# Splitting a router's column sums and residual products around its count, with later row waits, another PSUM bank and no zero products ahead of x

## The reference

```python
# layer 1 (called e1 in the kernel): RMS norm, experts of width 256
x = x + mixed @ w_out
x = x + _hier_moe(_rmsnorm(x, norm_ffn_g), ...)
# layers 2 and 3 (e2, e3): layer norms, experts of width 512
for i in range(2):
    ...
    y = concatenate([y_mix, y_mem], axis=-1) @ w_o[i]
    x = layer_norm(DEEPNORM_ALPHA * x + y, ln1_g[i], ln1_b[i])
    f = hierarchical_moe(x, w_rg[i], b_rg[i], w_re[i], b_re[i], w_gate[i], w_up[i], w_down[i])
    x = layer_norm(DEEPNORM_ALPHA * x + f, ln2_g[i], ln2_b[i])
# hierarchical_moe: best of 4 groups, best 2 of its 8 experts by logits x @ [w_rg | w_re];
# every token's output is the weighted sum of its two experts' silu(x @ gate) * (x @ up) @ down
```

## Time and profile before

| | us |
|---|---|
| median of 3 runs | 1717.15 |
| lowest, highest | 1714.5, 1717.75 |
| the profiled execution | 1714.65 |
| its span, first to last instruction | 1712.9 |
| PE busy in the span | 1601.9 (94%) |
| DVE, ACT, POOL busy | 522.1, 273.3, 35.7 |
| DMA | 570.23 MB, mean 333 GB/s |
| chain that ended last, by engine | PE 63%, DMA 30%, DVE 3% |

### The profile page before, as it was taken

How to read it: one execution, slowest core, us unless ns; L and a number is a source line. 1 busy time by engine, 2 the same in 40 slices (tenths; PEclk the granted TensorE clock), 3 DMA queues, 4 the chain that set the end, 5 groups by cost and what they waited for, 6 DMA issues and landing times.

```text
span 1712.9 us, 30730 instructions
## 1 busy us (share of the span) xinstructions
PE 1601.9 (94%) x12513; PEld 800.3 (47%) x12518; DVE 522.1 (30%) x1178; ACT 273.3 (16%) x545; POOL 35.7 (2%) x78
## 2 busy tenths in 40 slices
PE   8998998977699999999999999999899999999997
PEld 5486765643367553434333333674434333333332
DVE  6986333111048452112121111414542111111113
ACT  2303111000035220101010100223211010001011
POOL 4000000010000000000000000000000000000000
PEclk9999999989899999999999999999999999999999
DMA  6323459999984089999999999831389999999996
GB/s 249 136 111 147 166 217 410 421 421 420 421 367 160 34 312 422 422 422 422 421 422 422 422 422 422 373 133 66 148 334 421 422 422 422 422 422 422 421 422 256
DMA packets 79527, 570.23 MB, mean 333 GB/s; under 512 B 8878, under 2 KB 12390, under 8 KB 14566
## 3 DMA queue, kind: packets, MB, share of 16 engines
q1 hardware_dynamic: 77750, 563.41, 80.1%
q10 hardware_dynamic: 1712, 5.92, 0.9%
HBM read 568.24 MB, written 1.05 MB: 332 GB/s over the span
## 4 chain that ended last, share of the span: by engine, by line
PE 63%; DMA 30%; DVE 3%; issue 2%; ACT 1%; SPq 1%; POOL 0%; DVEq 0%; PEldq 0%; POOLq 0%; ACTq 0%
DMA space<-in_e_up 30%; PE psum L1092 20%; PE psum L1131 8%; PE psum L897 5%; PE psum L834 5%; PE psum L842 4%; PE psum L1144 4%; PE psum L1014 3%; PE psum L1456 2%; PE psum L1416 1%; PE psum L1001 1%; PE psum L886 1%; PE psum L1467 1%; PE psum L1356 1%; PE psum L1222 1%
## 5 line engine op out<-in xcount | busy, mean ns | idle before, releaser
L1092 PE MATMUL psum<-space 128*32 (+1 forms) x5056 | 524.1, 566 | 53.0 <-DMA space<-in_e_up 49.0
L1092 PEld LDWEIGHTS psum<-space 128*32 128x32 f32 x5056 | 168.4, 113 | 394.7 <-issue 386.7
L1131 PE MATMUL psum<-space 128*32 128x512 f32 (+1 forms) x2304 | 257.1, 597 | 6.3 <-DMA space<-in_e_down 6.3
L2151 DVE TENSOR_TENSOR space<-space,psum 128x512 f32<-128x512 f32 (+1 forms) x40 | 25.4, 635 | 581.6 <-PE psum L1092 581.6
L1144 PE MATMUL psum<-space 128*128 128x512 f32 x320 | 150.4, 613 | 0.0
L1131 PEld LDWEIGHTS psum<-space 128*32 128x32 f32 x2304 | 71.7, 110 | 162.5 <-issue 162.5
L834 PE MATMUL psum<-xT,space 128*128 128x256 f32 x448 | 98.5, 380 | 3.0 <-ACT xT L1520 1.0
L1144 PEld LDWEIGHTS psum<-space 128*128 128x128 f32 x320 | 54.2, 189 | 96.6 <-issue 71.8
L2158 DVE COPY space<-psum 128x512 f32<-128x512 f32 x40 | 27.7, 691 | 231.6 <-PE psum L1131 231.6
L834 PEld LDWEIGHTS psum<-xT,space 128*128 128x128 f32 x448 | 84.6, 190 | 15.9 <-issue 4.6
L1014 PE MATMUL psum<-space,xT 128*128 128x128 bf16 x1024 | 89.4, 219 | 0.0
(11 more groups left out here) (399 smaller groups left out, 1411.4 us busy)
## 6 DMA issues: line engine op xcount, KB each, us to landing
space<-in_e_up SPq DMA_DIRECT2D x160, 1024.0 KB, 20.2
space<-in_e_down SPq DMA_DIRECT2D x160, 1024.0 KB, 20.4
space<-in_e_gate SPq DMA_DIRECT2D x156, 1024.0 KB, 21.1
space<-in_stream SPq DMA_DIRECT2D x25, 2048.0 KB, 15.4
rows<-in_rows ACTq DMA_DIRECT2D x9, 512.0 KB, 8.8
rows<-in_e_gate SPq DMA_DIRECT2D x4, 1024.0 KB, 25.9
space<-in_stream SPq DMA_DIRECT2D x3, 1024.0 KB, 9.6
x_sb<-in_x SPq DMA_DIRECT2D x2, 512.0 KB, 4.0
```

The source lines that it names most:

```text
L1092: last = mm(psum[r, 5 + g, 0:FW], xg[:, u, k, r], w, start=(k == 0), stop=(k == KD - 1))
L1131: last = mm(psum[r, (4, 7)[half], :], hT[:, f, r], w, start=(f == 0), stop=(f == F - 1))
```

## The change

Five edits. (1) The zero products ahead of x and behind the first transposes are gone, and POOL clears no_sum after alpha_id and not first. (2) The gain rows' transpose goes to bank 7; the alternation of banks 0 and 1 shifts by one from f on. (3) In the router the residual products are issued two and two, the first two behind the first token half's norm; the first set of column sums stands between them, the second set behind the ranks; fewer zero products follow (none in e1, three in e2, seven as before in e3); PE waits for banks 5 and 6 after the first gather, not ahead of it; ACT copies the sums after the bfloat16 part. (4) `residual_norm` waits for the rows ahead of the first centring. (5) DVE clears wcomb and rank after the differences.

```diff
@@ plan @@
     for n in range(2):
         use2("u", n)
+    use(("gains",), 7)
...
-    use2("gains")
     use2("f")
@@ gpsimd @@
-        step(po.memset(no_sum[:, :], 0.0))
-        finish(po, "pool", "no_sum")
         step(po.memset(ident[:, :], 0.0))
...
         finish(po, "pool", "alpha_id")
+        step(po.memset(no_sum[:, :], 0.0))
+        finish(po, "pool", "no_sum")
@@ tensor, moe @@
-            after(pe, "pool", "alpha_id")
-            if e != "e1":
-                after(pe, "vec", e + "_tok")
-            for b in range(4):
+            def residual_start(b):
+
                 pe.wait_ge(bank_free[b], before_moe[e][b])
                 mm(psum[:, b, :], (ident if e == "e1" else alpha_id)[:, :], x_sb[:, b // 2, b % 2 * 512:(b % 2 + 1) * 512],
                    start=True, stop=False, skip_group_check=True)
+
+            def column_sums(c):
+
+                w = (routers[int(e[1])], wr_shift)[c]
+                for k in range(KD):
+                    last = mm(psum[:, plan[(e + "sums",)][0], c * NR:(c + 1) * NR], ones[:, :], w[:, k, :],
+                              start=(k == 0), stop=(k == KD - 1))
+                return last
+
+            after(pe, "pool", "alpha_id")
+            if e != "e1":
+                after(pe, "vec", e + "_tok0")
+            for b in range(2):
+                residual_start(b)
+            if e != "e3":
+                after(pe, "pool", f"router{int(e[1]) + 1}")
+                open_bank(pe, e + "sums")
+                column_sums(0)
+            if e != "e1":
+                after(pe, "vec", e + "_tok")
+            for b in range(2, 4):
+                residual_start(b)
             if e == "e3":
                 idle_products(0, 5)
-            else:
-                after(pe, "pool", f"router{int(e[1]) + 1}")
-                b = open_bank(pe, e + "sums")
-                for c, w in enumerate((routers[int(e[1])], wr_shift)):
-                    for k in range(KD):
-                        last = mm(psum[:, b, c * NR:(c + 1) * NR], ones[:, :], w[:, k, :], start=(k == 0), stop=(k == KD - 1))
-                close_bank(last, e + "sums")
...
             close_bank(last, e + "rank")
-            idle_products(1, 3 if e == "e1" else 7)
-            for b in range(4, 8):
+            if e != "e3":
+                close_bank(column_sums(1), e + "sums")
+            idle_products(1, {"e1": 0, "e2": 3, "e3": 7}[e])
+            for b in (4, 7):
                 pe.wait_ge(bank_free[b], before_moe[e][b])
...
             gather(0, 0)
             gather(0, 1)
+            for b in (5, 6):
+                pe.wait_ge(bank_free[b], before_moe[e][b])
@@ tensor, start @@
-        idle_products(7, 16)
...
-        idle_products(7, 3)
@@ scalar, moe @@
-            if e != "e3":
-                src = full(ac, e + "sums")
-                copy_out((e + "sums",), wr_sums[:, :], src[:, 0:2 * NR])
             if e != "e1":
                 for th in range(TH):
                     step(act(parts[0][th], x_sb[:, th, :], ACT.Copy))
                 finish(ac, "act", e + "_hi")
+            if e != "e3":
+                src = full(ac, e + "sums")
+                copy_out((e + "sums",), wr_sums[:, :], src[:, 0:2 * NR])
@@ vector, residual_norm @@
-            ve.wait_ge(flag(f"rows{a}"), 32)
...
                 if th == 0:
+                    ve.wait_ge(flag(f"rows{a}"), 32)
                     centred(a, th, whole)
@@ vector, moe @@
-            counted(ve.memset(wcomb, 0.0))
-            step(ve.memset(rank, -1.0))
             ve.wait_ge(small_sem, 16 * NSMALL)
...
             tell(e + "_d21")
 
+            counted(ve.memset(wcomb, 0.0))
+            step(ve.memset(rank, -1.0))
             step(ts(r_pen2, sel, -1.0, 1000.0, ALU.add, ALU.mult))
```

More of the change, by code:

```diff
@@ L518, in _build @@
                                                   "ln31_std0", "ln31_std1", "e3_ge", "e3_p2", "e3_hi", "e3_mid0", "e3_mid1", "ln32_std0", "ln32_squares1", "ln32_std1"],
-        "pool": ["no_sum", "ident", "c_zeros", "masks", "alpha_id", "powers_low", "tap_id", "router1", "router2", "router_done2", "router3", "tap_w", "spans", "router_done3"]}
+        "pool": ["ident", "c_zeros", "masks", "alpha_id", "no_sum", "powers_low", "tap_id", "router1", "router2", "router_done2", "router3", "tap_w", "spans", "router_done3"]}
     finished = {who: flag(who + "_finished") for who in milestones}
```

## The result

The changed kernel takes 1700.93 us (median of 4 runs, 1699.65 to 1702.79), the kernel before beside it 1716.2 (median of 4, 1714.5 to 1717.75): a ratio of 0.9912, 95% interval 0.9895 to 0.9929. It is 15.1 us faster (12 to 18), where 12.7 were forecast from the median of 1717.15 shown then, and 11.3 as the sum of the steps. Profile against profile, 1714.65 stands against 1699.65, and the spans differ by 15.0 us as well.

A forecast was written before the change was run, and what follows sets the result against it. TensorE's work ahead of each weight stream restart was taken to bound the kernel. Terms 1.8 + 1.0 + 0 + 3.4 + 5.1 = 11.3 us gave 1703.4 from the profile, 1705.9 from the median; forecast 1704.5, range 1699.5 to 1711.5.

The forecast's parts named there:

- What bounds it: Whole kernel: TensorE's time saved ahead of each weight stream restart counts one for one, time saved after it nothing.
- (b): Rival: the clock is kept everywhere, 14 us saved; 1700.7 to 1703 us; chance 0.10.
- the start: Before u: without the zero products u starts 3.5 us earlier; 1.8 us left after clock loss, ends 0.9 and 3.5.
- low-clock term: At the start: one spell at half clock costs u 1.7 us; bounds 0 and 2.6.
- The bank: Ahead of f: gains in bank 7 let f follow at once, without idle PE; 1.0 us.
- e1's router: First layer: removed zero products start step 0 earlier, but the queued weight load hides it; 0, bounds 0 and 1.1 us.
- e2's router: Second layer: the count waits for the selection, no longer for PE; 3.4 us, ends 2.5 and 3.7.
- e3: Third layer: residual sum without the rows' pause 4.5 us, router another 0.6; together 5.1, ends 4.2 and 5.6.
- (e): Rival: the clock stays low from the start through u, q and k; slower, up to 1722.6 us; chance 0.03.
- (c): Rival: the stream sets e2 and e3 anyway, only 2.8 us remains; 1712 to 1714 us; chance 0.05.
- (d): Rival: column sums behind the rank hold up the gather, e2 brings 1.4 us; 1706.5 to 1708 us; chance 0.05.
- (a): Rival: low clock eats the start and slows e2's sums and gather, 8.6 us saved; 1706 to 1708.6; chance 0.15.

The follow-up runs named there:

- e7: Changed kernel with eight more zero products behind the ranks in e1's and e2's routers; e1's logits to its last output product 238.60 us (238.55 without them).
- e8: Changed kernel with 24 more zero products in e1's router; e1's logits to its last output product 239.88 us (238.55 without them).
- the repeat of after: The changed kernel run and profiled again, unchanged; 1705.68 us.
- e9: Changed kernel with the gains' transpose back in the alternating banks, bank 7 not used; 1703.92 us, ratio 0.9925 to the kernel before.
- e6: Changed kernel with both sets of column sums ahead of the count again and the old number of zero products, residual products still split; 1700.02 us.
- e11: Changed kernel with DVE's two memsets back at the head of the routing chain; 1709.02 us.
- e3: As a run: changed kernel with the sixteen and three zero products back at the start and no_sum cleared first; 1704.81 us, ratio 0.9941 to the kernel before.
- e5: Changed kernel with the wait for the norm rows back at the top of residual_norm; 1708.52 us, ratio 0.9955 to the kernel before.

## Why the prediction was right, step by step

**What bounds it: right.** The forecast 1704.5 with a range to 1699.5 holds 1700.93, which lies within rival (b), 1700.7 to 1703, and not at the forecast. The sum was 11.3 us and the profiles differ by 15.0. Of the 3.7 between them 1.5 are the start, whose low-clock term stayed away, and 1.9 the attention, which the forecast didn't have; both hang on where the clock was low in the two profiled executions, so for the prediction they are luck. The rest is within 0.5. e7 and e8 show both halves of the argument, the cover in e1 and the pass-through in e2.

**The start: mechanism right, one term mis-sized.** 3.3 us for 3.5 (the transposes started at 7.37 for 7.25 and took 3.67 for 3.8). The low-clock term, 1.7 us, is the one that was mis-sized: it was nil in the profiled execution, and 0.8 us in the mean of ten. Its bounds, 0 and 2.6, held nine of ten. I took "one spell" because the rows showed whole spells; they did not show how often one falls on a given place. The Trainium skill (TensorE: Matmul & The Clock Gate, Part 1) says that the throttled state is the default and that activity releases it. The trace agrees: the sixteen transposes that come first now take 3.67 us, 1.91 when the zero products went ahead. What the prediction drew from it, that no part of the loss could be zero, holds for these transposes and not for u, which lost nothing in six of ten profiles.

**The attention: not forecast.** 1.9 of the 15.0. It goes with the granted clock (0.86 before, 0.89 after), and at least in part it is a draw: the repeat of after, at 0.85, has 0.35 us there. Without it, the first profile would have given 13.1.

**The bank: right**, 1.05 for 1.0, and the wait returns in e9.

**e1's router: right**, 0.15 for 0, though the saving there was larger than the 1.1 I counted: step 0 came 2.2 us earlier with respect to the logits (13.92 to 11.71), since the column sums behind the ranks also let the count come 1.7 earlier (6.84 to 5.14 us behind the logits; 6.92 in e6). I had looked only at the three zero products. Cover made the omission harmless.

**e2's router: right**, 3.6 for 3.4, by the route described: count by the selection, the copy 1.51 us behind it. The split of the residual products carries it, the column sums little, and part of what the split brings is the clock that the pause had cost. The low end, 2.5, was set too high: in three of ten profiles with the split (the repeat of after, e8, e11) a spell fell on the sums and the gather, and step 0 stood 16.45 to 16.63 us behind the logits, a gain of only 1.1 to 1.3 over the 17.77 of before. I had let the low clock delay the gather's start and had not counted that the gather itself then takes 5.39 us for 3.81. In a fourth (e3) it fell on the residual products and cost 0.4.

**e3: right**, 4.9 for 4.5 in the residual part (3.1 of pause, 1.75 of clock) and in the router exactly the 0.6: from the residual sum's end to step 0 it is 19.84 us before and 19.26 after (the 1.05 of the table less the 0.47 of the row above it). The memsets, which I counted as a gain of 0.24 at the selection and a loss of 0.3 behind it, are a net loss of 0.2. One part was weaker than I wrote: I treated half clock behind the pause as given; it is in three of four executions, so the saving is 3.1 always and 1.75 mostly. And the 0.6 of the router isn't kept in every execution: in three of the ten profiles with the split (e5, e8, e9) a spell there made it 20.2 to 21.2 us from the residual sum's end to step 0, where the three of before have 19.8 to 19.9.

**The rivals.** (e), a low clock through u, q and k, didn't happen; the longest loss in u was 3.1 us. (c) falls by the windows and by e7. (d), whose time should read 1705.4 to 1707.9 by the prediction's own terms, was right on one thing: when the clock is low behind the ranks, e2 brings about 1.3, near its 1.4. (a) describes executions like the repeat (1705.68) and e11, and (b) the first one: they are not rivals so much as the two ends of one kernel's scatter.

## What to carry to other kernels

Find where the weight stream restarts, and what it waits for: ahead of it each microsecond of TensorE counts in full, and behind a queued load that is still landing some are free in both directions (here 2.2 of gain and 1.65 of delay; of 5.1 of delay 3.8). Where an engine waits for several things at its first step, move each wait down to the first instruction that uses it; here that gave back a pause of 3 us and, mostly, 1.7 us of clock behind it. Put products of zeros only into waits that exist: here 5.78 us of them, begun 1.0 us ahead of the first half of x, held u up by 3.3; and where spells of low clock move between executions, read two profiles of a kernel before a term of 1.7 us is booked.

## What the runs showed of the hardware

- A spell at 1.2 GHz cost 1.7 to 1.75 us in the convolution part and in e3's residual sum and some 2.3 on e2's sums and gather, and u lost 1.5 to 3.1 us in four of ten profiles. Where it falls differs between executions of one kernel: enough for 1699.65 and 1705.68 us.
- The granted clock in the windows was 1.00 over the start of the second profile of after, though nine products took 3.47 us. At the start of a kernel the duration of the products has to be read, not the clock. In after:

```profile
12.00:17.00 5.00, 4.54 (x21) 4.05 (x22) 4.22 (x31) 0.47 (x2) 1.34 (x5) 1.00 1.16 340
```

There 21 products took 4.54 us (0.22 each), at the same recorded 1.00.

- A spell needs no long pause ahead of it. In the repeat of after the clock was low (0.62) between 605 and 610 us, where TensorE was busy all the time, with an idle of 0.66 us ahead of the count. Behind the 1.15 to 1.31 us of idle ahead of the unsplit residual products the clock was low in eight of eight, and without that idle in four of twenty; behind the 3 us pause in e3 it was low in three of four.
